# Reordering the first attention block, its latent up-projections, the opening and the S5 mixer of a two-block model on one core

## What is computed

```python
xn = rms_norm(h, norm_mix_pre); proj = xn @ w_in
# 12 heads of 64 in three groups: window 128 dilation 1, 512 / 4, 2048 / 16
o_a = mixer_dilated(qkv_a, pos) @ w_o_a    # softmax over the groups' log-sums weighs them
q  = rms_norm(q_c, q_norm) @ w_uq          # latent attention, 8 heads
kv = rms_norm(kv_c, kv_norm) @ w_ukv
mix = (sigmoid(..) * o_a + sigmoid(..) * o_b) @ w_out
```

## Time and profile before

| | |
|---|---|
| median of 3 runs | 1632.44 us (1631.73 to 1633.38) |
| the profiled execution's own time | 1624.21 us |
| its span, first to last instruction | 1622.4 us |
| mean granted TensorE clock | 0.969 |
| TensorE, VectorE, ScalarE, GpSimd busy | 1520.4, 811.5, 576.0, 283.9 us |
| HBM read | 124.82 MB, 79 GB/s over the span |

### The profile page before, as it was taken

The page is one execution under the profiler, slowest core; times in us unless marked ns, Lnnn a source line. Parts: engine busy times, 40 slices in busy tenths (PEclk is TensorE's granted clock), DMA queues, the critical chain, the costliest instruction groups (busy, mean ns, idle before and its releaser), DMA issues. The chain is left out here.

```text
span 1622.4 us, 18642 instructions
## 1 busy us (share of the span) xinstructions
PE 1520.4 (94%) x7560; PEld 1232.3 (76%) x7560; DVE 811.5 (50%) x1166; ACT 576.0 (36%) x902; POOL 283.9 (18%) x296
## 2 busy tenths in 40 slices
PE   7989899779999999999998999988799999999997
PEld 5878678676688888888886766776678888888885
DVE  4231544277765546434346776377856434324425
ACT  4222534335745423322235412285325222212212
POOL 0000000000032698000003265414312000000000
PEclk9999999999999999999999989989799999999998
DMA  4321221040033232232232212110012322322322
GB/s 176 102 80 56 78 78 46 23 135 20 1 117 101 82 104 82 100 104 96 86 130 62 78 53 78 59 53 27 1 53 79 104 80 102 104 98 85 104 91 78
DMA packets 38858, 129.25 MB, mean 80 GB/s; under 512 B 4676, under 2 KB 23004, under 8 KB 27380
## 3 DMA queue, kind: packets, MB, share of 16 engines
q1 hardware_dynamic: 38484, 127.93, 23.1%
q10 hardware_dynamic: 288, 0.12, 0.0%
HBM read 124.82 MB, written 3.17 MB: 79 GB/s over the span
## 5 line engine op out<-in xcount | busy, mean ns | idle before, releaser
L242 PE MATMUL bank<-xT_hi,ring_hi 128*128 128x512 f32 (+3 forms) x920 | 358.0, 389 | 19.8 <-ACT gates L1786 8.8
L223 DVE TENSOR_TENSOR ring_lo<-ring_raw,ring_hi 128x2048 fp32r<-128x2048 f32 (+3 forms) x115 | 265.9, 2315 | 192.6 <-ACT ring_hi L213 192.5
L242 PE MATMUL bank<-xT_lo,ring_hi 128*128 128x512 f32 (+3 forms) x920 | 353.7, 384 | 0.0
L242 PE MATMUL bank<-xT_hi,ring_lo 128*128 128x512 f32 (+3 forms) x920 | 353.5, 384 | 0.0
L213 ACT CAST ring_hi<-ring_raw 128x2048 fp32r<-128x2048 f32 (+3 forms) x115 | 212.9, 1853 | 240.9 <-DMA ring_raw<-in_w_ff 130.4
L242 PEld LDWEIGHTS bank<-xT_hi,ring_hi 128*128 128x128 f32 (+2 forms) x920 | 174.8, 190 | 62.1 <-ACT gates L1786 9.7
L242 PEld LDWEIGHTS bank<-xT_hi,ring_lo 128*128 128x128 f32 (+2 forms) x920 | 174.5, 190 | 34.8
L242 PEld LDWEIGHTS bank<-xT_lo,ring_hi 128*128 128x128 f32 (+2 forms) x920 | 175.0, 190 | 33.3
L242 PE MATMUL bank<-ring_hi,hid_hi 128*128 128x512 f32 x432 | 169.4, 392 | 4.0 <-DVE ring_lo L223 4.0
L242 PE MATMUL bank<-ring_lo,hid_hi 128*128 128x512 f32 x432 | 169.0, 391 | 0.0
L242 PE MATMUL bank<-ring_hi,hid_lo 128*128 128x512 f32 x432 | 169.0, 391 | 0.0
(11 more groups left out here) (496 smaller groups left out, 2129.1 us busy)
## 6 DMA issues: line engine op xcount, KB each, us to landing
ring_raw<-in_w_ff SPq DMA_DIRECT2D x30, 1024.0 KB, 4.8
ring_raw<-in_w_up SPq DMA_DIRECT2D x22, 1024.0 KB, 4.9
ring_raw<-in_w_proj SPq DMA_DIRECT2D x8, 1024.0 KB, 5.3
ring_raw<-in_w_gates SPq DMA_DIRECT2D x8, 1024.0 KB, 4.9
ring_raw<-in_w_fm SPq DMA_DIRECT2D x12, 512.0 KB, 4.9
ring_raw<-in_w_dn_a SPq DMA_DIRECT2D x6, 1024.0 KB, 4.9
ring_raw<-in_w_proj SPq DMA_DIRECT2D x8, 512.0 KB, 4.4
ring_raw<-in_w_out SPq DMA_DIRECT2D x4, 1024.0 KB, 5.0
```

What stands on the lines that cost most here:

```text
L223: k.nc.vector.tensor_tensor(k.ring.lo[:, g % SLOTS, 0:n], k.raw[:, g % SLOTS, 0:n], plain(k.ring.hi[:, g % SLOTS, 0:n]), ALU.subtract).the ...
L242: mm = k.nc.tensor.matmul(out, x, y, start=first and n == 0, stop=last and n == 3 * len(pairs) - 1)
```

## The change

- Opening: ScalarE casts chunk 0 before `high_part(0)`; its subtraction is done in halves by VectorE and GpSimd; VectorE does `low_part(0)` before the third mean. The pole constants go with tile 13 instead of 12. The first stage splits one chunk ahead at its end instead of two; `stage_turn` casts that chunk on ScalarE and subtracts it on GpSimd.
- The latents are no longer scaled before their transposes: their root is a factor in the copies of the up-projections' tiles. All key/value tiles there are copied by ScalarE.
- Attention: the dilated groups' 8 batches come first. Gates come whole in even rounds; ScalarE copies a round's gates and latent transposes ahead of the next pair's exponentials, and VectorE their low parts ahead of the maxima; splits follow the exponentials and maxima. The logarithm and four subtractions (for 24) go to the up-projections' stage, and SyncE's scratch stores wait for them.
- S5: units 0 to 5 are injected and projected in pairs, the instructions of two units interleaved; three buffers instead of two; the second unit of a pair uses banks 3 and 7; feature tiles use three banks.

```diff
@@ Opening
+            pe.wait_ge(self.low_pool.sem, 1)
@@ Opening.act
         square(1)
+        split_hi(k, act, 1)
+        high_part(0)
         square(2)
-        high_part(0)
-        split_hi(k, act, 1)
@@ Opening.pool
+            if t == 2:
+                pool.wait_ge(self.k.w_hi.sem, 1)
+                self.low_half(self.k.nc.gpsimd, 1).then_inc(self.low_pool.sem, 1)
@@ Opening.dve
         scale(1)
+        dve.wait_ge(k.w_hi.sem, 1)
+        self.low_half(v, 0).then_inc(k.w_split.sem, 1)
+        low_part(0)
         mean(2)
-        low_part(0)
         scale(2)
-        split_lo(k, dve, 1)
...
-            if j == 12:
+            if j == 13:
@@ stage_gemm
-            split_hi(k, act, end + LEAD)
+            split_hi(k, act, end + ahead)
@@ stage_turn
                 norms.pool(pool)
+                gates.split_by_pool(pool, gates.first + 1)
...
                 gates.keep_gate(act, 0)
-                norms.scale(act)
+                split_hi(k, act, gates.first + 2)
@@ stage_attention, ScalarE
+            for i in range(0, nb + 1, 2) if paired and beside.early else ():
+                beside.keep(act, i - 2)
+                beside.keep(act, i - 1)
+                if i < nb:
+                    exponentials(i)
+                    exponentials(i + 1)
+                beside.splits(split_hi, act, i - 2)
+                beside.splits(split_hi, act, i - 1)
+                if i < nb:
+                    evac("act", act, i)
@@ stage_attention, VectorE
+                if beside.early:
+                    beside.lows(dve, i - 2)
+                    beside.lows(dve, i - 1)
                 if i < nb:
                     maximum(i)
                     maximum(i + 1)
+                if beside.early:
+                    beside.splits(split_lo, dve, i - 2)
+                    beside.splits(split_lo, dve, i - 1)
@@ first_block
+    later = [x for n in range(6) for x in (("gate", 9 + n), ("turn", n))] + [("gate", 15)]
+    order = [("gate", n) for n in range(9)] + later
+    rounds = {0: (2,), 2: (3, 4), 4: (5,), 6: (6, 7), 8: (8,)}
+    rounds = {r: [("gate", n, half) for n in ns for half in range(2)] for r, ns in rounds.items()}
+    rounds.update({10 + 2 * n: [("gate", 9 + n, 0), ("gate", 9 + n, 1)] + ([("turn", n, 0)] if n < 6 else [])
+                   for n in range(7)})
...
+    stage_gemm(k, steps, evac_b, lambda j: "dve" if j % 2 and j < 8 else "act", act_each=mix.act, dve_each=mix.dve,
+               sync=mix.sync)
@@ Combine.sync
+        sp.wait_ge(self.ready.sem, self.ready.base + 4)
@@ Combine
+    def logs(self, act):
+        self.k.nc.scalar.activation(self.mx[:, :, :], self.ls[:, :, :], ACT.Ln).then_inc(self.logged.sem, 1)
@@ stage_proj2
+    BANKS = range(3)
+    BU = [((k.pb[3], k.pb[7]) if n in (1, 3, 5) else (k.pb[4], k.pb[5])) for n in range(8)]
...
+                for c in range(2):
+                    for n in units:
+                        q = 32 * (n % 4)
+                        mm = nc.tensor.matmul(BU[n][c][:, :], bT[q:q + 32, c, n // 4, :], uT[q:q + 32, n // 4, :],
+                                              start=True, stop=True, tile_position=(q, 0))
...
+                    if n in (3, 5, 7):
+                        project(n - 3, n - 2)
+                    if n == 8:
+                        project(6)
+                    if n in (0, 2, 4):
+                        inject(n, n + 1)
+                    if n in (6, 7):
+                        inject(n)
```

More of the change, by code:

```diff
@@ L511, in stage_gemm @@
 def stage_gemm(k, steps, evac, owner=None, act_each=None, dve_each=None, dve_tail=None, pool=None,
-               needs=(), closing=None, opening=None, begun=0, sync=None):
+               needs=(), closing=None, opening=None, begun=0, sync=None, ahead=LEAD):
     nc = k.nc
@@ L738, in squares, with root_of @@
                 n += 1
[L740 to L745, removed]
+    def root_of(self, part, t):
+        return self.parts[part][3][:, t:t + 1]
     def pool(self, pool):
@@ L828, in act, with lows @@
                 act.wait_ge(self.turned.sem, self.turned.base + n + 1)
-                k.nc.scalar.mul(dst.hi[:, f, :], self.bank((kind, n))[:, :], gain).then_inc(self.high.sem, 1)
+                self.k.nc.scalar.mul(dst.hi[:, f, :], self.bank((kind, n))[:, :], gain).then_inc(self.high.sem, 1)
             elif half:
                 self.keep_gate(act, n)
[L832 to L839, removed]
+    def lows(self, dve, r):
+        for kind, n, half in self.rounds.get(r, ()):
             if kind == "turn":
@@ L842, in dve, with splits @@
                 dve.wait_ge(self.high.sem, self.high.base + n + 1)
[L843 to L847, removed]
+                self.k.nc.vector.scalar_tensor_tensor(out=dst.lo[:, f, :], in0=self.bank((kind, n))[:, :], scalar=gain,
+                                                      in1=plain(dst.hi[:, f, :]), op0=ALU.mult,
+                                                      op1=ALU.subtract).then_inc(self.low.sem, 1)
+    def splits(self, split, eng, r):
+        if r == -1:
+            split(self.k, eng, self.first + 1 + LEAD)
+        for kind, n, half in self.rounds.get(r, ()):
+            if kind == "gate" and half and n % 2:
+                split(self.k, eng, min(self.steps[n][0] + 1 + LEAD, self.end + LEAD))
     def close(self):
@@ L990, in exponentials @@
                 e.then_inc(expd.sem, 1)
-            for i in range(0, nb + 1, 2) if paired else ():
+            for i in range(0, nb + 1, 2) if paired and beside.early else ():
[8 more added lines that the diff above has]
+                    evac("act", act, i)
+            for i in range(0, nb + 1, 2) if paired and not beside.early else ():
                 if i < nb:
@@ L999, in _ @@
                     evac("act", act, i)
-            for r in range(nb + 1, beside.steps_on_pe + 1) if paired else ():
-                beside.act(act, r)
+            if paired and not beside.early:
+                for r in range(nb + 1, beside.steps_on_pe + 1):
+                    beside.act(act, r)
             for i in range(nb + 1) if not paired else ():
@@ L1057, in _ @@
                     evac("dve", dve, i + 1)
-            for r in range(nb + 1, beside.steps_on_pe + 1) if paired else ():
-                beside.dve(dve, r)
+            if paired and not beside.early:
+                for r in range(nb + 1, beside.steps_on_pe + 1):
+                    beside.dve(dve, r)
             for i in range(nb + 2) if not paired else ():
@@ L2717 @@
 class FoxSide:
+    early = False
     def __init__(self, k, g):
```

179 lines of the change are left out of this document (97 added, 82 removed).

## The result

The changed kernel takes 1588.21 us (median of 4 runs, 1583.22 to 1592.91), the kernel before 1632.09 (4 runs, 1626.60 to 1633.38) in the same comparison: ratio 0.9729, 95% interval 0.9710 to 0.9748, or 43.9 us less. Forecast were 1595.4 and a range of 1586.5 to 1605. The two profiled executions lie 36.4 us apart (1624.21 and 1587.83), against a summed 37.0. The table gives the starts of the stages in these two; the shift grows where a stage became shorter.

What follows compares the result with a forecast made beforehand. The prediction took TensorE's one long row of matmuls (94% busy) as the bound: its idle, half-clock time and slots. Terms -1.0 -7.9 -6.4 -12.7 +1.1 -10.1 = -37.0 took the median from 1632.4 to 1595.4 us; range 1586.5 to 1605.

Steps and rivals of the forecast that it cites:

- opening and pole constants: Start and first stage: earlier first product, -1.0 us; VectorE's wait at the pole constants and half clock gone, -7.9.
- stage boundary: End of projection stage: idle 5.06 becomes 0.95 us and the half clock after it goes, -6.4 us.
- attention: First attention: waits for gate copies and half clock go, a new tail appears; 141.62 becomes 128.9 us, -12.7.
- up-projections: Up-projections' end: ScalarE's copy of the last key/value tile delays cast and subtraction, +1.1 us.
- S5: S5 stage: four paired slots saved, -7.5 us, and shorter half clock, -2.6; sum -10.1.
- The late rounds' waits (0.8): Attention: seven late rounds want the bank of the gate just before, costing 0.8 us in all.
- The tail: Attention's end: ScalarE's copies and cast, VectorE's subtraction and normalisations, block change; 5.5 us, 0.4 covered by mix, 5.1 idle.
- the owner of the tiles: Up-projections: all key/value tiles go to ScalarE, so the last cast starts later and the stage ends 1.1 us later.
- the half clock, put at 2.6: S5: half clock of 10.24 us at 954.8 shortens to 5 us, since full-width matmuls follow the project pair; -2.6 us.
- the two waits named: S5: waits of some 3 us before the second inject pair and before the first project pair (GpSimd).
- the 1589 to 1601 to which I gave 0.64: Whole kernel: the main forecast's span of times in us, given chance 0.64.
- My rival called better: Whole kernel: no half clock after S5's wait or at the start, and a short attention tail; 1588 us, chance 0.10.

Runs made afterwards that it cites:

- experiment 5: Changed kernel with only the pole constants moved back from tile 13 to tile 12: 1594.28 us (4 runs).
- Experiment 8: Changed kernel with only the opening as before (chunk 0 cast after the third square, subtracted by VectorE alone): 1589.19 us (4 runs).
- experiment 6: Changed kernel whose projection stage again ends only with chunk 14 cast and subtracted by VectorE, GpSimd's subtraction dropped: 1597.51 us (4 runs).
- experiment 7: Changed kernel with attention's gate and transpose copies after the next exponentials and VectorE's low parts after its maxima: 1620.13 us (5 runs).
- experiment 9: Changed kernel with the up-projections' key/value tiles again copied by ScalarE and VectorE in turn: 1582.97 us (2 runs).
- experiment 2: Changed kernel with S5 back to single units, two product buffers and the old banks and gate-row places: 1600.88 us (4 runs).
- experiment 11: Changed kernel with attention's and up-projections' last splits left to the next stage, plus S5's second inject pair a chunk later: 1594.90 us (5 runs).
- experiment 1: Changed kernel again, unaltered, beside the kernel before: 1587.94 us (5 runs) against 1631.41 (9 runs), ratio 0.9739.
- experiment 3: Changed kernel with the matmuls of each S5 pair issued unit after unit instead of alternately: 1589.70 us (4 runs).
- 4: Changed kernel with both units of each S5 inject pair read from the first unit's row group: 1594.75 us (2 runs).

## Why the prediction was right, and where not

| term | forecast | profiled executions |
|---|---|---|
| opening and pole constants | -8.9 | -9.7 |
| stage boundary | -6.4 | -6.3 |
| attention | -12.7 | -13.3 |
| up-projections | +1.1 | +0.8 |
| S5 | -10.1 | -10.7 |
| all else | 0 | +2.8 |
| sum | -37.0 | -36.4 |

**Pole constants.** Right by rows and by experiment 5 (7.6 for 7.9). The 0.8 by which the table's first line exceeds the forecast is clock at the start: TensorE's first products start 0.43 us apart from 17.9 to 22.6 in the kernel before, and from 17.5 to 20.8 here, which gives 1.0 us beside the 0.6 of the earlier start. Experiment 8 shows that this differs between executions.

**Opening.** First product at 16.70 for 16.4, 0.6 us sooner for 1.0; GpSimd's half 3.40 for 3.5. The slow end of my bounds, 6.4 us, did not come. GpSimd needed some 1.1 us more than the 2.3 estimated above, about as long as VectorE's half ran beside it (1.23). The Trainium skill (GPSIMD Engine Reference, Specifications) says that GpSimd's SBUF interfaces are shared, with contention when VectorE's instruction has two SBUF inputs; the trace agrees with that in kind, though no run here has the two halves apart.

**Boundary.** Idle 0.92 for 0.95, and no half clock at the gates; shown by experiment 6 too.

**Attention.** 128.31 us for 128.9, out of parts that cancel. The late rounds' waits (0.8) did not come. The tail was put at 5.1 idle and is 3.68, because the last mix covered 1.5 us of ScalarE's copies and cast, not 0.4. And 3.4 us at a granted clock of 0.50 from 178.0, which I had not counted, took 1.7. In eight other executions without it the attention takes 126.8 to 127.1. That the term needs the copies ahead of the exponentials is shown by experiment 7; I had priced the placement and the order together and did not see that the placement without them would lose.

**Up-projections.** +0.8 for +1.1. The step that gave it (the owner of the tiles) was mis-sized: it is 0.3, by experiment 9. The other 0.6 of the idle's growth from 4.45 to 5.38 stands in no term of the forecast: by the rows of experiment 9 it is VectorE's longer copies and their later start.

**S5.** The sum and its division were right: nothing before GpSimd's unit 1 (it cost 1.5 us, as 6.8 us of half clock now follow the first inject and put VectorE's unit 0 later), and 12.2 behind it for 10.1 forecast. The mis-sized term is the half clock, put at 2.6 and worth 4.7 by experiment 2. Of the two waits named, that for VectorE came (2.5); the one for GpSimd did not, since TensorE arrives within 0.14 us of that event, and experiment 11 shows it at full length (6.7). The Trainium skill (TensorE: Matmul & The Clock Gate, Measured speedup vs the span model) has 2.38x for three column tiles, by which a pair would be a quarter longer; here a project pair took as long as a single one (953.23 to 955.07, 1.84 us, against 1.83), and the measurement decides.

**The level.** The forecast of 1595.4 lies 7.2 above the result, and nearly all of that is the step from the profiled execution to the median. I took the difference of the profiled executions as that of the medians. The execution of the kernel before that I read lies 8.2 below its median and was shorter than all 26 of the experiments' comparisons, that of the changed kernel 0.4 below its own. Its late mixers took the short form of experiment 1; the long form's 9.7 us would account for the 8.2, but no trace of a long execution of the kernel before exists. The row for all else lies in stages that nothing touches, where the half clock fell otherwise: 0.75 of the 2.8 us ahead of S5 (6.8 instead of 3.4 us of it there), 2.1 behind, where the part after the late mixers is 3.1 us longer (441.52 for 438.37) with 6.8 us more half clock at its start. So that the profiled difference met the sum to 0.6 us is in part luck: the changed stages gave 2.2 more than forecast, and the untouched ones took 2.8. The range held with 1.7 us to spare; the median lies 0.8 below the 1589 to 1601 to which I gave 0.64. My rival called better, at 1588, named the right number for a partly wrong reason: the half clock behind S5's wait did go, but the tail was 1.4 us short and not 2.3, and the rest came from the level.

## What to carry over

Ask of each wait which event ends it, and then what the same event will hold once that wait is gone; S5's opening stretch did not fall below 45.1 us under any order of TensorE's work tried here, since another chain sets it. Work for the stage behind that is put at a stage's end, on its copying engines, is paid for as idle and again as half clock; leaving it to the stage behind was worth 6 to 7 us at one boundary and 6.5 at two others together. Where two edits share a queue, price each without the other: the attention's edits together saved 13 us, and without the early copies they cost 20.

## What the runs showed that I had not expected

- Matmuls in different row groups do not start in program order (experiment 3): with unit n's two products ahead of unit n+1's, both units' first products started within 13 ns. The Trainium skill (TensorE: Matmul & The Clock Gate, The mechanism) says that matmuls start and end strictly in order; the trace of this kernel shows otherwise for these fp32 products.
- One stretch that no edit touches, the late mixers, takes 68.5 or 78.2 us with the same instructions, at a granted clock of 0.80 or 0.61 (78.2 in the profiled executions of experiments 1 and 3, 71.9 to 72.3 in those of 2, 4 and 11, 68.3 to 68.6 in the other eight). That difference alone is about as large as the spread of the runs of one kernel.
- GpSimd subtracts 1024 wide in 3.40 us in the opening and 2048 wide in 4.58 behind the first stage, for which VectorE takes 1.23 and 2.29: the narrow one, beside VectorE's own half, is far slower for its width.
